# Two branch projections computed output tile by output tile over both of their weight units

## What is computed

```
o_a = dsa_attention(q_a, k_a, v_a, q_i, k_i, w_i)        # 256 x 512
o_b = moba_attention(q_b, k_b, v_b)                      # 256 x 512
merged = (sigmoid(gate_a) * (o_a @ w_br_dsa)             # w_br_*: 512 x 1024
          + sigmoid(gate_b) * (o_b @ w_br_moba))
x = x + gt_m * (merged @ w_out)                          # w_out: 1024 x 1024
h = rms_norm_2(x, g_ffn_norm) * (1.0 + sc_f) + sh_f
g_ff, u_ff = split(h @ w_gate_up)
x = x + gt_f * ((silu(g_ff) * u_ff) @ w_down)
```

## Time and profile before

| | |
|---|---|
| median of 3 runs | 1470.17 us (1469.43 to 1471.49) |
| span of the profiled execution | 1468.2 us |
| TensorE matmuls busy | 1446.1 us, 98% |
| VectorE busy | 1056.6 us, 72% |
| ScalarE busy | 700.0 us, 48% |
| instructions | 28465 |

### The profile page before, as it was taken

One profiled execution on the slowest core, in us unless ns is written; L12 is line 12 of the kernel. 1 busy time (PEld: TensorE's weight loads), 2 busy tenths in 40 slices (PEclk: granted clock), 3 DMA queues, 4 the chain that ended last, 5 costly groups with the idle time before them and its releaser, 6 DMA issues. The chain is left out here.

```text
span 1468.2 us, 28465 instructions
## 1 busy us (share of the span) xinstructions
PE 1446.1 (98%) x11585; PEld 1406.6 (96%) x11585; DVE 1056.6 (72%) x1439; ACT 700.0 (48%) x910; POOL 29.0 (2%) x58
## 2 busy tenths in 40 slices
PE   8999999999999999999999999999999999999999
PEld 8999999999999999999999889999987899999999
DVE  6766779777667786677878768767887777876652
ACT  6544353454443454443554655443436766544431
POOL 0000100000001000001000000001000000000000
PEclk9999999999999999999999999999999999999999
DMA  9555835437447644458343226647633436365540
GB/s 324 220 187 186 268 149 201 172 106 267 172 172 249 239 173 172 171 196 288 128 173 124 78 70 246 227 173 268 234 115 135 145 139 231 131 228 185 184 173 30
DMA packets 42538, 269.09 MB, mean 183 GB/s; under 512 B 4768, under 2 KB 5920, under 8 KB 13520
## 3 DMA queue, kind: packets, MB, share of 16 engines
q1 hardware_dynamic: 33984, 240.31, 45.1%
q0 software_dynamic: 7312, 26.44, 5.5%
q10 hardware_dynamic: 1152, 1.05, 0.2%
HBM read 266.73 MB, written 1.05 MB: 182 GB/s over the span
## 5 line engine op out<-in xcount | busy, mean ns | idle before, releaser
L418 PE MATMUL ps<-x_hi,w_hi 128*128 128x272 f32 (+2 forms) x2296 | 661.8, 288 | 6.7 <-DVE x_lo L1447 1.9
L420 PE MATMUL ps<-x_hi,w_lo 128*128 128x272 f32 (+2 forms) x2296 | 651.8, 284 | 0.0
L419 PE MATMUL ps<-x_lo,w_hi 128*128 128x272 f32 (+2 forms) x2296 | 651.7, 284 | 0.0
L2024 ACT ACTIVATE w_hi<-raw_weights 128x2048 fp32r<-128x2048 f32 x219 | 416.9, 1912 | 291.6 <-PE ps L420 289.0
L1174 DVE TENSOR_TENSOR w_lo<-raw_weights,w_hi 128x2048 fp32r<-128x2048 f32 x193 | 439.7, 2288 | 143.8 <-ACT w_hi L2024 143.3
L418 PEld LDWEIGHTS ps<-x_hi,w_hi 128*128 128x128 f32 x2296 | 433.1, 189 | 10.8 <-DVE x_lo L1380 2.5
L419 PEld LDWEIGHTS ps<-x_lo,w_hi 128*128 128x128 f32 x2296 | 433.3, 189 | 0.7
L420 PEld LDWEIGHTS ps<-x_hi,w_lo 128*128 128x128 f32 x2296 | 433.1, 189 | 0.0
L418 PE MATMUL ps<-a_hi,w_hi 128*128 128x272 f32 x592 | 169.6, 286 | 0.0
L419 PE MATMUL ps<-a_lo,w_hi 128*128 128x272 f32 x592 | 169.6, 286 | 0.0
L420 PE MATMUL ps<-a_hi,w_lo 128*128 128x272 f32 x592 | 169.6, 286 | 0.0
(11 more groups left out here) (259 smaller groups left out, 1543.9 us busy)
## 6 DMA issues: line engine op xcount, KB each, us to landing
raw_weights<-w_units SPq DMA_DIRECT2D x226, 1024.0 KB, 4.9
mod_w<-mod_units POOLq DMA_DIRECT2D x48, 512.0 KB, 5.5
raw_weights<-w_units SPq DMA_DIRECT2D x4, 256.0 KB, 5.8
raw_weights<-w_units SPq DMA_DIRECT2D x2, 512.0 KB, 9.2
out<-h ACTq DMA_DIRECT2D x8, 128.0 KB, 1.9
h<-x_in SPq DMA_DIRECT2D x2, 272.0 KB, 4.1
h<-x_in SPq DMA_DIRECT2D x1, 544.0 KB, 8.0
tab<-tables POOLq DMA_DIRECT2D x1, 512.0 KB, 7.9
```

The lines of the kernel that those rows point to most:

```text
L418: pe.matmul(dst, wh, hi, start=start, stop=False)
L419: pe.matmul(dst, wh, lo, start=False, stop=False)
L420: return pe.matmul(dst, wl, hi, start=False, stop=stop)
L2024: act.activation(w_hi[:, u % RING, :], raw[:, u % RING, :], ACT.Copy).then_inc(S["hi_ready"], 1)
```

## The change

Both calls of k_outer for br_dsa and br_moba become calls of a new function, by_tile. It waits at its start until both units of the stage are split. Then it goes through the eight output tiles; for each it waits for the bank and does all four input tiles, two of each unit, twelve matmuls in a row. tile_done is raised after each tile. weights_used, which lets go of the first unit, is raised after that unit's last product in the last tile (m = 7). w_out and down4 stay with k_outer. The orders of ScalarE, VectorE and SyncE are the same as before.

```
+            def by_tile(st, xs, a_base):
+
+                pe.wait_ge(S["lo_ready"], st.u0 + st.units)
+                for m in range(8):
+                    wait_bank(st, st.t0 + m)
+                    for n in range(st.units):
+                        for kk in range(2):
+                            k = 2 * n + kk
+                            if m == 0:
+                                pe.wait_ge(S["a_ready"], a_base + k + 1)
+                            ins = three_pass(ps[:, st.bank(st.t0 + m), 0:st.T], (st.u0 + n) % RING, (kk * 8 + m) * P,
+                                             xs[0][:, k, 0:st.T], xs[1][:, k, 0:st.T], k == 0, k == 2 * st.units - 1)
+                        if m == 7 and n < st.units - 1:
+                            ins.then_inc(S["weights_used"], 1)
+                    ins.then_inc(S["tile_done"], 1)
+
...
-            k_outer(stages["br_dsa"], (o2_hi, o2_lo), A0["w_in"])
-            k_outer(stages["br_moba"], (o2_hi[:, 4:8, :], o2_lo[:, 4:8, :]), A0["w_in"] + 4)
+            by_tile(stages["br_dsa"], (o2_hi, o2_lo), A0["w_in"])
+            by_tile(stages["br_moba"], (o2_hi[:, 4:8, :], o2_lo[:, 4:8, :]), A0["w_in"] + 4)
```

## The result

Over 16 runs of each kernel the median went from 1471.77 us (1469.43 to 1476.62) to **1479.93 us** (1475.20 to 1483.88), 8.2 us more. The ratio of runs is 1.0047, with a 95% interval of 1.0036 to 1.0057, that is 6.9 us, between 5 and 8. The forecast was 1479.6 us, with a range of 1476.0 to 1482.4; it rests on 9.4 us more, which is above that interval. Single executions of one kernel spread over 7 to 9 us here and over up to 13 us in later runs, so in what follows times are read from the profiles wherever a profile can tell more than a median.

A forecast was written before the change was run, and what follows sets the result against it. TensorE, busy 98% of the span, was taken as the bound. Waits of 6.7 us, pace 0.4 and clock 1.3 + 1.0 made 9.4 us: span 1477.6, median 1479.6 us, range 1476.0 to 1482.4.

The forecast's parts named there:

- first stop, before br_moba: Before br_moba: TensorE idles 4.53 us because br_dsa's products, which free its banks, stand behind C0's delayed split on VectorE.
- first matmul after it: At br_moba's start: the first matmul after a stop is followed after 0.19 us instead of 0.11, costing 0.08 us.
- growth of the gap before w_out: Before w_out: z_hi stands behind C2's split, which waits for B0's later release; 2.1 us more idle.
- slow pace in br_moba: In br_moba: a stop can put matmuls on 117.7 instead of 113.3 ns until B0's release; 0.4 us taken.
- clock, first stop: After the stop before br_moba: granted clock falls to half for a spell; 1.3 us taken, bounds 0 and 3.4.
- clock, second stop: After the stop before w_out: granted clock falls to half for a spell; 1.0 us taken, bounds 0 and 1.7.
- the wait for both units at the start: At br_dsa's start: by_tile needs A1's w_lo, split 4.6 us ahead; at br_moba B1's is done; cost nothing.
- w_out's banks: In w_out: br_moba's last product frees tiles 6 and 7 near 1259.2, needed at 1260.8; covered.
- C2, C3 and SyncE's loads: In w_out: C2 and C3 split by about 1267, third unit needed at 1270; loads 4.8 us later cost nothing.
- the three tails: Earlier narrow-matmul tails after short stops: clock fell to 0.51 at 869 and 1057 us, kept 1.00 at 312 us.
- The waits alone, without the clock: Rival: both stops come but the clock stays up, 6.7 to 7.1 us more, 1476.9 to 1477.3 us; chance 0.18.
- The pace that turns the other way: Rival: the stop puts w_out, up4 and down4 on the fast pace, saving 10.2 us, 1466.7 us; chance 0.04.

The follow-up runs named there:

- moving z_hi: Changed kernel with ScalarE's four z_hi written ahead of the w_hi split of C2; stretch 27.97 us, ratio to the kernel before 1.0055.
- the late release alone: Kernel before, matmul order untouched, only weights_used of A0 and B0 raised on the 93rd of 96 matmuls; stretch 31.60 us, ratio 1.0084.
- the run with the products first: Changed kernel with VectorE's four products of br_dsa ahead of the w_lo split of C0; stretch 24.66 us, ratio to the kernel before 1.0027.
- the run with br_dsa alone: Kernel before with by_tile for br_dsa only, br_moba still k_outer; stretch 29.68 us, ratio to the kernel before 1.0049.

## Why the prediction was right, point by point

| term | forecast | measured in the profile after |
|---|---|---|
| first stop, before br_moba | 4.53 | 1246.17 - 1241.66 = 4.51 |
| first matmul after it | 0.08 | 0.20 - 0.11 = 0.09 |
| growth of the gap before w_out | 2.1 | 3.01 - 1.01 = 2.0 |
| slow pace in br_moba | 0.4 | 0.0 |
| clock, first stop | 1.3 | 1.6 |
| clock, second stop | 1.0 | 0 |
| sum | 9.4 | 8.2 |

**The waits.** The clock follows them: it was low behind a stop or at its end, and where all stops were removed it stayed at 1.00 from br_dsa's first matmul to TensorE's last. In the profile after it was at 1.00 all through the first stop (1241.55 to 1246.17), so it did not cause that stop. Place, size and cause were right, and each is shown: moving the products takes away the first stop and leaves the second as it was, moving z_hi takes away the second, with the old 0.9 us, and leaves the first, and the late release alone makes both in the kernel before. In the two profiles of the changed kernel and the first of the kernel before, the 212.7 us behind the stops did not move, so the stops add up there; in an execution of before with 209.6 us the difference would have been 3 us larger.

**What was costed at nothing** stayed at nothing: the wait for both units at the start (no idle time before br_dsa's first matmul), w_out's banks, C2, C3 and SyncE's loads (no wait in w_out or up4; up4's first split starts 6.0 us after w_out, 1267.67 - 1261.67, as before).

**The pace.** This term was wrong in its reason: the stop did not put br_moba on the slow pace. Its last eight microseconds have 72 matmuls, as the fast pace has. The one stop that the prediction went by was one draw: in the run with the products first, w_out was fast behind a stop of 3 us (211.1 us to the end is 209.5 and 1.6 for the clock).

**The clock.** The spell at the first stop came and cost 1.6 us, what 3.4 us at half cost; it was never absent in five profiles with a first stop. At the second stop it was taken at 1.0 and did not come in the profiles of the changed kernel; over all runs with a gap of 3.0 to 3.4 us it came in two of five, and in none of the three that had the first stop as well. By these counts, known only now, the terms would have been 1.6 to 1.8 and 0.6. The prediction's reading of the three tails, two that fell and one that did not, took for a difference between places what differs between executions of one kernel. The two errors of clock and pace and the rounding of the second stop make the 1.2 us between 9.4 and 8.2. The median came out 0.3 us from the forecast since the median of before in the 16 runs lies 1.6 us above that of the first three (1471.77 against 1470.17). Counted from the same base the forecast was 1.2 us too high against the profile and 2.5 against the ratio; that closeness is luck.

**The rivals.** The waits alone, without the clock, are excluded for the two profiled executions, which both have a spell behind the first stop. The pace that turns the other way exists (w_out and down4 took 3.2 us less in several runs), but not in up4, where the prediction had priced 7.0 us. So it could not have outweighed the stops.

## What to carry to other kernels

When a release moves later, look not for who needs the released thing soon, but for what is written behind the instruction that waits for it: here C0 was not needed until br_moba's 96 matmuls were over (10.9 us at 113.3 ns), C2 not until two units of w_out were (11.3 us at 117.7 ns), and the loss came from four products and four copies in line behind their splits. A finer order of production gains only if the consumers' written orders are moved with it; here the finer order in br_moba alone, with one moved line on ScalarE, made of a loss of 0.5% a gain of perhaps 0.15%. For differences of a few microseconds under a noise of as many, measure a stretch between two named instructions in the profile: it repeated to 0.01 us between profiles that had the same stops and the same low clock.

## What the runs showed of the hardware that was not expected

**Two paces of one instruction stream.** Three-pass matmuls of 256 columns run at 113.3 or 117.7 ns from start to start, for hundreds in a row, with the granted clock at 1.00 in both. Without a stop ahead of w_out (four profiles) the pace was 113.3 each time; behind the gap of 1.0 us it was 117.7 in two profiles of the kernel before and 113.3 in a third and in the run with br_dsa alone; behind the gaps of 3.0 to 3.4 us it was 117.7 in four of five. And down4 mostly has the pace of w_out, but with by_tile for br_moba alone it had 113.3 (211.9 us to the end is 209.5, 1.6 for the clock and 0.8 for w_out alone). What chooses it is open. It was not tried whether a stop of another length or other operands change the odds.

**How readily the clock falls.** Half clock began within 1.1 us of br_moba's first matmul, or during the stop before it, after all five stops of 4.5 to 4.9 us. It came after two of five stops of 2.9 to 3.3 us and after none of four gaps of 0.9 us. It lasted 3.4 us, once 6.8. The Trainium skill (TensorE: Matmul & The Clock Gate, section "HAM oscillation — how this bites in real kernels") has the mechanism, a long wait that leaves the next burst cold; these runs agree with it for the stops of 4.5 to 4.9 us, five of five; behind those of 2.9 to 3.3 us it came in two of five. Those two are the runs without a first stop; in the three with one, whose low clock had ended over 8 us before the second stop, it stayed at 1.00. Whether that is chance or a consequence was not tried.
